# First mixer of a two-layer decoder on one core: transposed input, stationary dt weights, running sums spread by DMA, output weights held back, a side projection moved one unit later

## The reference, cut to what matters

```python
proj = rms_norm(h, norm_w) @ in_w
z, xbc, dt, q_mem = split(proj, [1536, 2560, 24, 512])
xbc = silu(causal_depthwise_conv(xbc, conv_w, conv_b))   # 20 blocks of 128 channels
dt = softplus(dt + dt_bias); a = -exp(a_log)
# per chunk of 128 tokens (2) and group of 6 heads (4):
acum = cumsum(dt * a)
decay[l, s] = exp(acum[l] - acum[s])  for s <= l
y = (C B^T * decay) (x dt) + (C state) * exp(acum); state = B^T (x dt to_end)
y = rms_norm_per_group((y + d_skip * x) * silu(z)) * gnorm_w
m = memory_cross_attention(q_mem, mem, ...)
h = h + concat(y, m) @ out_w
```

## Time and profile before

| | |
|---|---|
| median of three runs | 1397.09 us (1397.0 to 1401.43) |
| the profiled execution, its own time | 1401.78 us |
| span of its instructions | 1400.0 us |
| TensorE busy | 1244.3 us (89%) |
| VectorE, ScalarE, GpSimd busy | 271.7, 206.3, 33.3 us |
| DMA | 458.78 MB, mean 328 GB/s |

### The profile page before, as it was taken

The page is one execution under the profiler, slowest core; times in us unless marked ns, Lnnn a source line. Parts: engine busy times, 40 slices in busy tenths (PEclk is TensorE's granted clock), DMA queues, the critical chain, the costliest instruction groups (busy, mean ns, idle before and its releaser), DMA issues. The chain is left out here.

```text
span 1400.0 us, 15283 instructions
## 1 busy us (share of the span) xinstructions
PE 1244.3 (89%) x6130; PEld 627.3 (45%) x6130; DVE 271.7 (19%) x679; ACT 206.3 (15%) x490; POOL 33.3 (2%) x42
## 2 busy tenths in 40 slices
PE   6999999989999999769687998999999999657685
PEld 6875875444444446223232566454444444212221
DVE  3542452031111110000002155031111111100001
ACT  3124233120000000000002145130000000000001
POOL 0001210000000000000000011000000000000000
PEclk9999999999999999879898999999999999888897
DMA  9543307569999998999999722439999999999994
GB/s 380 186 155 120 121 0 298 213 234 423 421 426 423 423 425 330 427 419 427 424 425 374 273 101 83 188 139 415 419 424 425 424 425 423 426 424 427 423 424 171
DMA packets 94666, 458.78 MB, mean 328 GB/s; under 512 B 7040, under 2 KB 7040, under 8 KB 61696
## 3 DMA queue, kind: packets, MB, share of 16 engines
q1 hardware_dynamic: 94592, 457.75, 80.1%
HBM read 456.67 MB, written 1.05 MB: 327 GB/s over the span
## 5 line engine op out<-in xcount | busy, mean ns | idle before, releaser
L1402 PE MATMUL bank<-own,e_xg 128*64 128x512 f32 (+1 forms) x1272 | 271.2, 634 | 39.6 <-DMA extra<-in_w_up 10.4
L1402 PE MATMUL bank<-late,e_xg 128*32 128x512 f32 (+1 forms) x648 | 165.2, 646 | 16.7 <-DMA late<-in_w_gate 8.3
L1402 PEld LDWEIGHTS bank<-own,e_xg 128*64 128x64 f32 (+1 forms) x1272 | 79.3, 130 | 203.4 <-issue 203.3
L1411 PE MATMUL bank<-own,e_turned 128*64 128x512 f32 (+1 forms) x592 | 133.2, 699 | 35.5 <-DMA own<-in_w_down 21.6
L1294 DVE TENSOR_TENSOR e_hid<-e_silu,bank 128x512 f32<-128x512 f32 x24 | 16.5, 688 | 506.6 <-ACT e_silu L1345 506.6
L1411 PE MATMUL bank<-late,e_turned 128*64 128x512 f32 (+1 forms) x392 | 91.2, 668 | 19.0 <-DMA late<-in_w_down 10.0
L1377 PEld LDWEIGHTS bank<-e_pick,xs 128*128 128x128 f32 x768 | 92.3, 197 | 21.8 <-issue 18.0
L1377 PE MATMUL bank<-e_pick,xs 128*128 128x128 f32 x768 | 98.7, 284 | 3.5 <-DVE e_pick L1241 3.5
L1345 ACT ACTIVATE e_silu<-bank 128x512 f32<-128x512 f32 x24 | 14.3, 598 | 543.0 <-PE bank L1402 543.0
L1402 PEld LDWEIGHTS bank<-late,e_xg 128*32 128x32 f32 (+1 forms) x648 | 46.1, 131 | 96.9 <-issue 96.8
L1394 PE MATMUL bank<-e_y,e_gates_T 128*128 128x512 f32 x192 | 86.5, 593 | 1.4 <-ACT e_gates_T L1353 1.4
(11 more groups left out here) (341 smaller groups left out, 1129.2 us busy)
## 6 DMA issues: line engine op xcount, KB each, us to landing
own<-in_w_gate SPq DMA_DIRECT2D x83, 1024.0 KB, 13.6
own<-in_w_up SPq DMA_DIRECT2D x76, 1024.0 KB, 12.0
own<-in_w_down SPq DMA_DIRECT2D x74, 1024.0 KB, 13.0
late<-in_w_down SPq DMA_DIRECT2D x49, 1024.0 KB, 11.8
late<-in_w_up SPq DMA_DIRECT2D x41, 1024.0 KB, 13.5
late<-in_w_gate SPq DMA_DIRECT2D x40, 1024.0 KB, 13.6
own<-in_a_in_w SPq DMA_DIRECT2D x18, 1024.0 KB, 12.0
extra<-in_w_up SPq DMA_DIRECT2D x11, 1024.0 KB, 13.4
```

Of the source, the lines that this page charges most:

```text
L1402: ins = pe.matmul(bank[q * T:(q + 1) * T, :], self.xg[:, at:at + T], cut(tile(q), k=4)[:, k, :], start=(half == 0 and k == 0), stop=(half ...
L1411: ins = pe.matmul(self.b_down[out][q * T:(q + 1) * T, :], self.turned[:, at:at + T], cut(tile(q), j=2)[:, j, 512 * out:512 * out + 512], s ...
```

## The change

- The host hands in x a second time, transposed (`xT`). The transposes of the input go. ScalarE scales the raw transposed x by the norm's weights (`xTw`), and `conv` 0 to 3 project that; VectorE multiplies their results by 1/rms afterwards (`raw`). The squares are summed by a unit `ss` (8 matmuls with ones stationary, 256 tokens moving), 1/rms is made for all partitions (`rb`: scale, ScalarE's square root, reciprocal, 128x256), and two VectorE instructions make the normalized `xnT` (128x1024 each) for the later units.
- dt: the weights, padded to 32 columns, are stationary (`dtp`: 8 matmuls of 256 tokens into four groups of 32 partitions), then two small matmuls with `dt_sum` add the groups and turn the result (`dt`, now behind `conv` 9).
- The constants are cut in two loads, the first with what the start needs, and padded from 2080 to 2176 columns (the tensors `h`, `xs`, `own`, `late`, `extra` lie behind them). The order of the first loads is new; tiles 1 to 4 go ahead of `mem` and `x`.
- The `A` units go from TensorE. A unit `acT` (behind `ac`) makes the running sums with heads in partitions; ScalarE stores them to HBM (`acum_rows`, 48 x 128) and loads three rows of them at a time, spread to 128 partitions, into `E`: four such loads ahead of loop 0, then two for step i+2 when `yd` i is done (i from 0 to 5). VectorE subtracts in place.
- SyncE waits for `yd` 5 before it issues tile 11, the first of the output weights, and so for all behind it.
- `SIDE` becomes `[NU - 3, NU - 2]`: the first side projection stands ahead of unit 9.

```diff
+DT_ROWS = 32
-SIDE = [NU - 4, NU - 2]
+SIDE = [NU - 3, NU - 2]
...
-        order = [("xT", i) for i in range(4)] + [("dt", 0)]
-        order += [("conv", j) for j in range(NCONV)]
-        order += [("z", 0), ("xtok", 0), ("xtok", 1), ("xtok", 2), ("bt", 0), ("ac", 0), ("z", 1), ("xtok", 3), ("xtok", 4), ("xtok", 5)]
+        order = [("conv", 0), ("conv", 1), ("ss", 0), ("conv", 2), ("conv", 3), ("dtp", 0)]
+        order += [("conv", j) for j in range(4, 10)] + [("dt", 0)] + [("conv", j) for j in range(10, NCONV)]
+        order += [("z", 0), ("xtok", 0), ("xtok", 1), ("xtok", 2), ("bt", 0), ("ac", 0), ("acT", 0), ("z", 1), ("xtok", 3), ("xtok", 4), ("xtok", 5)]
...
+        pe_order = [key for key in order if key[0] != "A"]
+        U = Units(c, pe_order, freed, holds)
...
         def _(sp):
-            for t in range(NT):
-                sp.dma_start(cut(c.h, t=NT)[:, t, :], g["x"][0, t * P:(t + 1) * P, :]).then_inc(ld_x[t], 16)
-            sp.dma_start(c.small[:, :], g["small"]).then_inc(ld_small, 16)
-            for n in range(2):
+            sp.dma_start(c.small[:, 0:FIRST_SMALL], g["small"][:, 0:FIRST_SMALL]).then_inc(ld_first, 16)
+            for half in range(2):
+                at = slice(4 * half * SEQ, 4 * (half + 1) * SEQ)
+                sp.dma_start(xT[:, at], g["xT"][:, at]).then_inc(ld_xT[half], 16)
+                c.load_mixer_half(sp, 0, half)
+            sp.dma_start(c.small[:, FIRST_SMALL:], g["small"][:, FIRST_SMALL:]).then_inc(ld_small, 16)
+            for n in range(1, 5):
                 c.load_mixer_tile(sp, n)
...
-            for n in range(2, TILES_A):
+            for n in range(5, TILES_A):
+                if n == TILES_A - 4:
+                    sp.wait_ge(c.units_done, U.at["yd", 5] + 1)
...
         def _(act):
+            for k in range(KD):
+                act.wait_ge(ld_xT[k // 4], 16)
+                act.activation(cut(xTw, k=KD)[:, k, :], cut(xT, k=KD)[:, k, :], ACT.Copy, scale=c.f("a_norm", k, k + 1)).then_inc(s["xw_ev"], 1)
+            act.wait_ge(s["rb_dve"], 1)
+            act.activation(rb[:, :], rb[:, :], ACT.Sqrt).then_inc(s["rb_act"], 1)
+            def load_decays(st):
+                for i in (2 * st, 2 * st + 1):
+                    ch, gr = steps[st]
+                    row = SSD_HEADS * ch + HG * gr + 3 * (i % 2)
+                    rows = acum_rows[row:row + 3, :].rearrange("(o r) l -> o (r l)", o=1)
+                    act.dma_start(E[i % 4][:, :], rows.broadcast_to([P, GW])).then_inc(e_loaded[i % 4], 16)
...
+                elif kind == "acT":
+                    U.wait_done(act, key)
+                    act.activation(acT, bank[0:NT * SSD_HEADS, 0:P], ACT.Copy).then_inc(s["acT_ev"], 1)
+                    act.wait_ge(s["acT_ev"], 1)
+                    act.dma_start(acum_rows, acT).then_inc(s["acum_stored"], 16)
...
+                    if i == 3:
+                        act.wait_ge(s["acum_stored"], 16)
+                        for st in range(2):
+                            load_decays(st)
...
+                elif kind == "yd" and i < 6:
+                    U.wait_done(act, key)
+                    load_decays(i + 2)
...
         def _(pe):
+                elif kind == "dtp":
+                    pe.wait_ge(s["xn_dve"], 2)
+                    for k in range(KD):
+                        q = DT_ROWS * (k % 4)
+                        ins = pe.matmul(out[q:q + DT_ROWS, 0:SEQ], cut(c.f("dt_w"), k=KD)[:, k, :], cut(xnT, k=KD)[:, k, :],
+                                        start=(k < 4), stop=(k >= 4))
+                elif kind == "acT":
+                    pe.matmul(out[0:NT * SSD_HEADS, 0:P], adt[:, :], c.f("tri"), start=True, stop=True).then_inc(c.units_done, 1)
-                elif kind == "A":
-                    ch, gr = steps[i // 2]
-                    for hh in range(3):
-                        hd = HG * gr + 3 * (i % 2) + hh
-                        ins = pe.matmul(out[:, hh * P:(hh + 1) * P], cut(adt, t=NT)[:, ch, hd:hd + 1].broadcast_to([P, P]),
-                                        c.f("tri"), start=True, stop=True)
...
         def _(dve):
+            def norm_x():
+                U.wait_done(dve, ("ss", 0))
+                dve.tensor_scalar(rb[:, :], U.bank(("ss", 0))[:, 0:SEQ], 1.0 / D, EPS, ALU.mult, ALU.add).then_inc(s["rb_dve"], 1)
+                dve.wait_ge(s["rb_act"], 1)
+                dve.reciprocal(rb[:, :], rb[:, :]).then_inc(s["rb_dve"], 1)
...
+                    dve.tensor_tensor(cut(xnT, k=KD)[:, k, :], cut(xTw[:, :], k=KD)[:, k, :], spread_mid(rb[:, :], 4), ALU.mult).then_inc(s["xn_dve"], 1)
...
+                    if i < 4:
+                        step(dve.tensor_tensor(raw[i], bank[:, 0:SEQ], rb[:, :], ALU.mult))
...
                 elif kind == "A":
-                    U.wait_done(dve, key)
+                    dve.wait_ge(e_loaded[i % 4], 16 * (i // 4 + 1))
```

More of the change, by code:

```diff
@@ L56 @@
 OVER_ROUNDS = 4
[L59 to L65, removed]
+FIRST_FIELDS = [("a_norm", KD), ("ones", P), ("conv_w", NCONV * 4), ("conv_b", NCONV), ("dt_w", KD * DT_ROWS), ("dt_sum", SSD_HEADS),
+                ("dt_bias", SSD_HEADS), ("a_log", SSD_HEADS)]
+FIELDS = FIRST_FIELDS + [
+    ("ident", P), ("tri", P), ("iota", SEQ), ("band_prev", P), ("band_cur", P), ("index8", EG), ("cos", NT * 16), ("sin", NT * 16),
+    ("mem_norm0", KD), ("mem_norm1", KD), ("kv_norm", KD), ("b_norm", KD), ("ffn_norm0", KD), ("ffn_norm1", KD), ("ffn_rows0", KD),
+    ("ffn_rows1", KD), ("gnorm", INNER // P), ("d_skip", SSD_HEADS), ("sinks", Q_HEADS),
+    ("route_b0", NG + NE), ("route_b1", NG + NE), ("route_w0", KD * (NG + NE)), ("route_w1", KD * (NG + NE))]
+FIELDS += [("rest", -sum(w for _, w in FIELDS) % P)]
+FIRST_SMALL = sum(w for _, w in FIRST_FIELDS)
 AT = {}
@@ L641, in mixer_a @@
         yt = c.xs[:, 4 * GW:5 * GW]
-        cbm = [sb(f"cbm{i}", P) for i in range(2)]
+        cbm2 = sb("cbm", 2 * P)
+        cbm = [cbm2[:, P * i:P * i + P] for i in range(2)]
         xw = [acc[:, i * GW:(i + 1) * GW] for i in range(2)]
         sq = xw
+        xT, xTw, rb = c.memT1, c.xs, cbm2
+        squares, raw, dtT = c.extra, [xbcT[:, (8 + i) * SEQ:(9 + i) * SEQ] for i in range(4)], c.extra[:, 7 * SEQ:8 * SEQ]
+        acT = qT[0:NT * SSD_HEADS, 0:P]
         state, ex, pTs = xbcT[:, 0:4 * GW], [xbcT[:, 4 * GW + 512 * i:4 * GW + 512 * i + 512] for i in range(2)], xbcT[:, 4 * GW + 1024:4 * GW + 1536]
@@ L741, in _ @@
         def _(act):
[L742 to L744 removed]
+            act.wait_ge(ld_first, 16)
+            act.activation(c.norm_r[:, 6:7], c.f("ones", 0, 1), ACT.Sqrt)
+            for k in range(KD):
[9 more added lines that the diff above has]
+                    act.dma_start(E[i % 4][:, :], rows.broadcast_to([P, GW])).then_inc(e_loaded[i % 4], 16)
             for key in order:
@@ L879, in _ @@
                     U.wait_free(pe, key)
-                if kind == "xT":
-                    if i == 0:
-                        pe.wait_ge(ld_small, 16)
-                        pe.wait_ge(s["x_dve"], 6)
-                    norm_T_units(c, pe, out, i)
+                if key == ("conv", 0):
+                    for k in range(KD):
+                        if k % 4 == 0:
+                            c.wait_job(pe, ("mixer", 0, k // 4))
+                        pe.wait_ge(s["xw_ev"], k + 1)
+                        ins = pe.matmul(out[:, 0:256], c.cols_at(0, k)[:, 0:P], cut(xTw, k=KD)[:, k, :], start=(k == 0), stop=(k == KD - 1))
+                    ins.then_inc(c.units_done, 1)
+                elif kind == "ss":
+                    pe.wait_ge(s["sq_dve"], 2)
+                    project(c, pe, out[:, 0:256], lambda k: c.f("ones"), lambda k: cut(squares, k=KD)[:, k, :])
                 elif kind == "memT":
@@ L1028, in _ @@
                 elif kind == "conv":
-                    step = chain(s["conv_dve"], 4 * i)
+                    step = chain(s["conv_dve"], conv_done(i))
                     U.wait_done(dve, key)
+                    if i == 4:
+                        dve.wait_ge(ld_small, 16)
                     if i >= 3:
```

81 lines of the change are left out of this document (50 added, 31 removed).

## The result

| | before | after |
|---|---|---|
| median of 20 runs each | 1398.2 us (1395.07 to 1401.67) | 1399.94 us (1397.82 to 1404.08) |
| ratio to before | | 1.0017, interval 1.001 to 1.0025 |
| span of the profiled execution | 1400.0 us | 1398.3 us |

The account below looks back on a forecast made before the run. TensorE was taken to bound the mixer and the DMA stream the experts; 8.3 + 10.4 - 1.6 + 7.5 - 0.1 = 24.5 us off the median 1397.1 gave 1372.6 us, range 1364 to 1384.

Parts of the forecast that it names:

- start: Up to z 0: the new start brings z 0 earlier by 8.3 us, bounds 5.5 and 9.3.
- A units less stalls: Eight steps of the mixer: 10.4 us go with the A units, less 1.6 us of stalls on the spread loads.
- output weights held back: End of the mixer: output weights waiting for yd 5 still land before TensorE needs them, so it costs nothing.
- side projection: Layer 0's experts: moved to unit 9, it closes the DMA hole from 530 to 547 us; 7.5 us, bounds 4 and 8.
- constants: Padding adds 0.05 MB, 0.1 us; moving the tensors behind by 384 bytes was taken as nothing.
- alignment: Rival, expert stream: the constants' row becomes a multiple of 256 bytes and speeds up the stream, up to 6 us: 1366; chance 0.04.
- Chain 5.9 to 7, stall 0.4: Loop 7: the spread load, sharing engines with the output weights, and its subtractions take 5.9 to 7 us, stalling 0.4.
- Passing on: Mixer to end of kernel: nothing between runs on its own clock, so the mixer's saving arrives at the end in full.
- slow spread loads: Rival, eight steps: late spread loads take the place of the A units, stalls some 7 to 15.7 us: 1378 to 1387; chance 0.13.
- The checks named beforehand: Trace signs: z at 85 us; VectorE waits over 3 us in loops 3, 5, 6; DMA share below 0.9 in layer 0's experts.

Follow-up runs that it names:

- e4: The changed kernel with 32 more columns of padding in the constants, 2208 in all: 1383.02 us against 1399.94 for the changed kernel.
- e5: e4 with the output weights held until the last two spread loads have landed, instead of until yd 5 is done: 1377.39 us, ratio 0.9851.
- e3: The kernel before with SIDE alone changed to [NU - 3, NU - 2]: 1391.69 us, ratio 0.9944.
- e10: The kernel before with an unused SBUF tensor of 32 columns behind the constants: 1410.48 us, before 1398.06.
- e7: The kernel before with an unused SBUF tensor of 96 columns behind the constants: 1409.99 us, before 1398.36.
- e12: The kernel before with an unused SBUF tensor of 112 columns just ahead of the ring's slots: 1409.31 us, before 1396.14.
- e9: e4 with the A units back on TensorE and the store, spread loads and acT gone: 1383.33 us, ratio 0.9902.

## Why the prediction was wrong

| term of the sum | forecast | measured |
|---|---|---|
| start | 8.3 | 7.9 |
| A units less stalls | 10.4 - 1.6 = 8.8 | 1.8; 0.0 in e4, 8.65 in e5 |
| output weights held back | 0 | in the line above |
| side projection | 7.5 | 7.7 in e3 alone |
| constants | -0.1 | -15.5; -16.9 by the medians |
| sum | 24.5 | 1.9, or 0.5; the spans differ by 1.7, the medians by -1.7 |

The constants' term is the difference between the changed kernel and e4 from the first scatter to the end, (1398.3 - 313.26) - (1383.9 - 314.35), which leaves e4's longer stall out; by the medians it is 1399.94 - 1383.02. Executions of one kernel scatter by a few us, so the sum can't agree more closely than that, and some 2 us stay open by the medians.

**The start was right**, term by term nearly. The first matmul came at 8.70 us for 8.1, the wait inside conv 0 was 0.17 for 0.4, and `dtp` took 1.07 us for the 0.9 allowed, so its groups do run side by side. The reciprocal took 1.75 us for 2.0.

**The side projection was right** in place, size and in passing on to the end.

**"It moves every tensor behind them by 384 bytes. No row isolates it; I take nothing"** is the step that failed, and it alone turned a gain into none: with 128 bytes more (e4) the same change gains 16 us. Two errors are in it. The first is of sign. The rival on alignment had the row's length go from 128 over a multiple of 256 to a multiple, and so the stream speed up. But a place is a base and lengths. With the base of 16512 the ring lay at a multiple of 256 before and 128 beside it after. Nothing in the profile shows the base, but the kernel's allocation does, and the prediction left it out. The second is of size. I bounded the effect by the 223 us in each layer in which the DMA is the limit, 6 us. It costs 15 to 17, and the milestones say where. From the first scatter of layer 0's experts to the last the changed kernel takes 749.96 - 313.26 = 436.7 us and e4 742.7 - 314.35 = 428.35; in layer 1 it is 425.11 against 419.05. That is 8.35 and 6.06 us, 1.9% and 1.4% of *all* of the expert time, though units 0 to 7 are spaced 29.45 us in every kernel. In these units TensorE uses 12 jobs of 1.05 MB in 29.45 us, 427 GB/s, a little more than either stream brings. So it must live on the ring's reserve, and a slower stream leaves a smaller one. No run shows the reserve itself, but the debt falls due at unit 8: there the changed kernel needs 40.4 us from scatter to scatter (559.87 - 519.43) and e4 36.5 (556.99 - 520.52).

For the kernel before the same displacement costs less, 8.7 us of span in e10 (1408.7 against 1400.0) and 8.9 to 13.2 by the medians, since the stop at its side projection gives the stream time to catch up: from 530 to 547 us e10 moves 320 GB/s where before moves 236, so that e10 is only 3.8 us behind at the start of layer 1's experts and 8.7 at the last unit. That's one more reason why the effect has to be measured on the changed kernel too.

By the Trainium skill, DMA: Bandwidth & Descriptors, How a descriptor splits into AXI transactions, a transaction starts at a multiple of 256 bytes, so that the first one of a descriptor that doesn't begins at the multiple below, and the bytes ahead of the start still cost beats. The prediction's estimate by that page, 1.5%, agrees in size with the runs (424 to 417 GB/s, 1.7%; the 8 KB packets alone 1.2%), and so does the sign, once the addresses are right. The runs add that it holds for the SBUF side of a load (HBM is the same in e7 to e12), and that the price of 3 to 4 ns a packet is the same for 64, 128 and 192 bytes. By beats of 32 bytes, as the page counts them, 8 KB would cost 2, 4 and 6 of them on top of 256; no such steps are seen.

**"Chain 5.9 to 7, stall 0.4" in loop 7** is the second step that failed, and with it "So it costs nothing" of the weights held back. I had seen that the load shares the engines with the output weights "which start at that very moment", and gave that and ScalarE's squares 1 to 2 us together. And against the late loads I had that "these have their own" queue; with it the later of the two loads took 8.1 us all the same. Measured are 6.0 and 8.1 us from issue to landing for 3.2 in the median, and the chain from the end of `yd` 5 (179.25) to `sc` 1 (189.50) is 10.25 us. What I had missed beside the size is who waits. I had looked at `yd`, and written that on ScalarE only "the copies of the next unit stand behind the two issues". But ScalarE's exponentials wait for the loads as well, both of them, and `mk` 1's copy stands behind these. So the second load counts, and its waiter is not `yd` 6 but `sc` 1, which comes earlier. No term for these loops had the clock in it. 5.66 us of idle time and 2.5 us at the slow clock are 8.2 us for the 0.4 forecast, and that is what the line of the A units lacks (8.8 - 1.8 = 7.0). In loops 0 to 6 TensorE idled 0.24 us in all, 1.2 forecast, which about makes the line's difference. e5 and e9 show it from both sides: without the collision the A units are worth 8.65 us, which is the forecast, and without the spread loads the output weights cost nothing.

**Passing on was right for the most part.** e5 has the place and the hold mended. By the medians it is 21.0 us faster than before, where the prediction has 24.5: most of it arrives, and 3.5 us stay open. That its span, 1375.3 us, meets the forecast of 1375.5 is luck, as the profiled execution of before took 3.6 us more than the median. Within the traces e5 is 15.6 us ahead at the first scatter of layer 0's experts and 22.4 at that of layer 1's.

Of the rivals, "slow spread loads" had the mechanism (a landing 2 us and more longer) for all loops, where it is one; "alignment" had the lever with the wrong sign. The checks named beforehand tell them apart: the DMA share was 1.02 from 530 to 547 us (0.90 was the alarm for the side term), z 0 was in place, VectorE waited over 3 us for a spread load once, at 185 us, and not in loops 3, 5 and 6. What I had no check for was GB/s at an unchanged DMA share.

## What to carry to other kernels

When a change resizes or adds a tensor in SBUF, work out the absolute place of every tensor behind it that large transfers write, with the allocator's base, and keep it a multiple of 256 bytes. In a kernel whose DMA share is 1, compare GB/s and not the share, before anything else is read: 1.7% over the whole stream cancelled three real savings.

A small transfer on the critical path mustn't be released by the same event as a burst of large ones; let the burst wait until the small one has landed. And for a late transfer list every engine that waits for it, with what stands behind that instruction in each program: the stall shows at the first of these, on whatever engine.

## What the runs showed of the hardware

- A load whose place in SBUF isn't a multiple of 256 bytes moves 413 to 418 GB/s where one that is moves 421 to 425, at full DMA share, and 64, 128 and 192 bytes over are alike. In the first 12 us of the changed kernel most 2 KB and 4 KB packets into such places took 84 and 159 ns, as before, and so did the 2 KB packets of e12; why the price begins only later is open.
- A broadcast load of 192 KB lands in 3.2 us on ScalarE's queue, and in 6.0 and 8.1 us when seven loads of 1 MB are issued on SyncE's in the same moment. A queue of its own doesn't protect it.
- The slow clock behind an idle stretch can cost as much as the stretch: after 5.66 us idle in the changed kernel it added 2.4 us, after 5.34 us in e4 it added 4.6 (8.81 and 10.96 us, start to start, for work that took e5 6.38). The granted clock was 0.62 and 0.50 in the window from 190 to 196 us. After e5's idle 1.22 us it stayed at 1.00.
- Matmuls into four groups of 32 partitions with 256 tokens moving overlap: 16 records of `dtp` took 1.07 us, 16 of a conv unit 3.62.
